# Expert rows added into h by scatters: a hybrid attention and mixture-of-experts block on one core

## The reference, cut to what matters

```
h = x + token_mixer(rms_norm(x, norm1_w), ...)
u = rms_norm(h, norm2_w)
# best of 4 groups, then the best 2 of its 8 experts; gate = softmax of the 2 scores * group weight
y[token, n] = (silu(u @ w_gate[e]) * (u @ w_up[e])) @ w_down[e]      # e: expert n of the token
h = h + sum over n of gate[token, n] * y[token, n]
out = rms_norm(h, final_norm_w)
```

## Time and profile before

| | |
|---|---|
| median of 3 runs | 1945.99 us (1945.32 to 1946.11) |
| profiled execution: its own time | 1948.25 us |
| profiled execution: span of the records | 1946.3 us |
| mean granted TensorE clock | 0.958 of full |
| mixer, about | 0 to 1009 us |
| routing, about | 1009 to 1063 us |
| experts | 1063 to 1863 us |
| last stage | 1863 to 1946 us |
| data moved by DMA | 379 MB, 195 GB/s over the span |

### The profile page before, as it was taken

One profiled execution on the slowest core, in us unless ns is written; L12 is line 12 of the kernel. 1 busy time (PEld: TensorE's weight loads), 2 busy tenths in 40 slices (PEclk: granted clock), 3 DMA queues, 4 the chain that ended last, 5 costly groups with the idle time before them and its releaser, 6 DMA issues.

```text
span 1946.3 us, 28769 instructions
## 1 busy us (share of the span) xinstructions
PE 1780.1 (91%) x10562; PEld 1267.3 (65%) x10563; DVE 572.6 (29%) x1111; ACT 498.9 (26%) x1189; POOL 216.1 (11%) x285
## 2 busy tenths in 40 slices
PE   7999999999999999999855999999999999999920
PEld 3566666566665666656634777888878778787710
DVE  1333233333233332433335111111111111111157
ACT  0434332343333342433310111111111111111113
POOL 0000001001011010110002000000000000000045
PEclk9999999999999999999976999999999999999965
DMA  9631133321333312333126789788998899898867
GB/s 322 188 109 61 59 97 108 108 83 36 97 108 108 104 39 73 108 108 108 64 90 235 273 290 325 267 299 308 322 316 296 299 314 329 286 332 303 281 221 319
DMA packets 231525, 379.01 MB, mean 195 GB/s; under 512 B 13715, under 2 KB 118180, under 8 KB 231492
## 3 DMA queue, kind: packets, MB, share of 16 engines
q1 hardware_dynamic: 220548, 340.14, 51.4%
q0 software_dynamic: 10944, 38.41, 5.9%
HBM read 282.04 MB, written 96.47 MB: 194 GB/s over the span
## 4 chain that ended last, share of the span: by engine, by line
PE 39%; DVE 4%; issue 4%; DMA 2%; ACT 1%; POOL 0%; SPq 0%; DVEq 0%; ACTq 0%; POOLq 0%
PE bank L1106 12%; PE bank L1131 12%; PE bank L1095 12%; PE bank L1120 1%; DMA out<-oc 1%; PE bank L1063 1%; DVE hT L1177 1%; DVE oc L1284 1%; DVE column L953 0%; DVE hc L1272 0%; DVE hc L1274 0%; ACT sg L1140 0%; DMA wts<-y_dram,dest 0%; DVE place L953 0%; PE bank L351 0%
## 5 line engine op out<-in xcount | busy, mean ns | idle before, releaser
L283 PE MATMUL bank<-w_in_sb,uT 128*128 128x512 f32 (+1 forms) x1024 | 381.7, 526 | 5.6 <-DMA w_in_sb<-w_in_in 5.6
L283 PEld LDWEIGHTS bank<-w_in_sb,uT 128*128 128x128 f32 x1024 | 177.3, 193 | 175.4 <-issue 168.5
L1095 PEld LDWEIGHTS bank<-xT,wts 128*128 128x128 f32 x2048 | 253.2, 194 | 28.9 <-issue 22.4
L1095 PE MATMUL bank<-xT,wts 128*128 128x128 f32 (+2 forms) x2048 | 258.7, 286 | 8.5 <-issue 6.6
L1106 PE MATMUL bank<-xT,wts 128*128 128x128 f32 (+2 forms) x2048 | 247.9, 282 | 0.0
L1106 PEld LDWEIGHTS bank<-xT,wts 128*128 128x128 f32 x2048 | 245.0, 191 | 0.0
L1131 PE MATMUL bank<-wts,hT 128*128 128x512 f32 x512 | 233.5, 599 | 3.8 <-DVE hT L1177 3.8
L431 PE MATMUL bank<-w_out_sb,mixT 128*128 128x512 f32 x512 | 224.2, 596 | 0.8 <-ACT mixT L508 0.8
L1177 DVE TENSOR_TENSOR hT<-bank,sg 128x256 f32<-128x256 f32 x128 | 54.3, 424 | 444.4 <-PE bank L1106 444.4
L431 PEld LDWEIGHTS bank<-w_out_sb,mixT 128*128 128x128 f32 x512 | 96.6, 191 | 116.9 <-issue 116.9
L1131 PEld LDWEIGHTS bank<-wts,hT 128*128 128x128 f32 x512 | 92.1, 190 | 105.6 <-issue 105.6
(11 more groups left out here) (212 smaller groups left out, 1714.6 us busy)
## 6 DMA issues: line engine op xcount, KB each, us to landing
wts<-w_gate_in SPq DMA_DIRECT2D x32, 2048.0 KB, 9.9
wts<-w_up_in SPq DMA_DIRECT2D x32, 2048.0 KB, 8.9
wts<-w_down_in SPq DMA_DIRECT2D x32, 2048.0 KB, 10.9
y_dram<-nought SPq DMA_DIRECT2D x96, 512.0 KB, 6.0
y_dram<-y SPq DMA_DIRECT2D x32, 512.0 KB, 9.7
x_sb<-x_in SPq DMA_DIRECT2D x17, 512.0 KB, 4.0
w_in_sb<-w_in_in SPq DMA_DIRECT2D x4, 2048.0 KB, 12.8
h_sb<-x_in SPq DMA_DIRECT2D x16, 512.0 KB, 6.3
```

The lines of the kernel that those rows point to most:

```text
L283: m = pe.matmul(bk[name][:, col:col + hi - lo], uT[:, k, :], w_in[:, k, lo:hi], start=k == 0, stop=k == KD - 1)
L1095: m = pe.matmul(G[m_ % 2][:, 0:w], wg[:, k, m_ * P:(m_ + 1) * P], xT[:, k, 0:w], start=k == 0, stop=k == KD - 1)
```

## The change

- Expert results no longer go through `y_dram`. ACT and VectorE scale by the gate of each slot (`gatec`, copied by ACT from `weight`) while they copy PSUM to `y`, and Pool adds the rows into h in DRAM with two indirect DMAs that accumulate (`put_back`). Empty slots add to spare rows behind h. One expert's scatters are waited for before the next one's go out (`scattered`), and that also frees `y`. The next expert's gather now follows the scatter in Pool's program.
- Routing makes two more tables per slot: `put` (the destination row) and `weight` (the gate). Pool writes the token products to a second tensor `column_t`, then multiplies `column` by the gates, four operations more; PE gets a second group of 32 matmuls and one more spread.
- `clear_y` is gone (two stores clear the spare rows), and so is the early load of h.
- The last stage loads h in four pieces after the last scatter has landed, normalises in place and stores.
- `sg` and `hT` are 160 columns wide in the main pass. Step 1 of the next expert's transposes stands before the down projection with step 0.
- Start: the bias of `qk` is loaded right behind the first `w_in` block, x of tile 1 behind the `v` block, five constants behind the `g` block, and six (with `alibi`) after all of `w_in`; their users wait for them where they need them.

```diff
+            if lo == C_QK:
+                sp.dma_start(b_tm[:, 0:C_V], A["b_in"][0:1, 0:C_V].to_broadcast([P, C_V])).then_inc(sem("b_qk_loaded"), 16)
             if lo == C_V:
-                for dst, src in [(b_tm[:, 0:C_LR], A["b_in"][0:1, 0:C_LR].to_broadcast([P, C_LR])),
+                sp.wait_ge(sem("xn_ready"), 1)
+                sp.dma_start(x[:, :], A["x"][P:2 * P, :]).then_inc(sem("x_loaded"), 16)
+            if lo == C_G:
...
+        for dst, src in [(sinks[:, :], A["swa_sinks"].to_broadcast([P, HB])),
+                         (gnorm[:, :], A["gla_norm_w"].to_broadcast([P, DV])),
+                         (cums[:, :, :], A["c_cums"]), (cind[:, :], A["c_cind"]),
+                         (causal[:, :], A["c_causal"]),
+                         (alibi[:, :, :], A["c_alibi"])]:
+            sp.dma_start(dst, src).then_inc(sem("late_consts"), 16)
...
-    def clear_y(sp, i):
-
-
-        blocks = scratch["y"].rearrange("(b p) (r c) -> b p r c", p=P, c=128)
+    def clear_spare(sp):
+
+        spare = scratch["h"][SEQ:SEQ + SPARE, :].rearrange("(b p) (r c) -> b p r c", p=P, c=128)
         src = nought[:, None, :].to_broadcast([P, D // 128, 128])
-        n = NE // NT
-        for m in range(n):
-            for b in (2 * (n * i + m) + 1, 2 * NE + 2 * (n * i + m), 2 * NE + 2 * (n * i + m) + 1):
-                dst = blocks[b] if isinstance(b, int) else blocks[bass.ds(b, 1)].rearrange("o p r c -> (o p) r c")
-                sp.dma_start(dst, src).then_inc(sem("y_cleared"), 16)
-
-    FIRST, CONSTS, W_OUT = 5 * 16, 11 * 16, 7 * 16
+        for b in range(SPARE // P):
+            sp.dma_start(spare[b], src).then_inc(sem("spare_cleared"), 16)
...
+            m = pe.matmul(bank[2][:, 0:NCOL], place[:, g, :], column_t[:, g, :], start=g == 0, stop=g == 2 * NT - 1)
+        m.then_inc(sem("slot_sums"), 1)
+        pe.wait_ge(sem("spread_args"), 1)
+        pe.matmul(bank[3][:, 0:NE], rep[:, 0:P], idx_f[:, :], start=True, stop=True).then_inc(sem("slot_sums"), 1)
+        for g in range(2 * NT):
+            if g % PART == 0:
+                pe.wait_ge(sem("columns_ready"), (2 * NT + g) // PART + 1)
+            m = pe.matmul(bank[6][:, 0:NCOL], place[:, g, :], column[:, g, :], start=g == 0, stop=g == 2 * NT - 1)
+        m.then_inc(sem("slot_sums"), 1)
+        pe.wait_ge(sem("spread_args"), 2)
+        pe.matmul(bank[7][:, 0:2 * NE], rep[:, 0:P], spread[:, :, :].rearrange("p a b -> p (a b)"), start=True, stop=True)\
+            .then_inc(sem("slot_sums"), 1)
...
+        pairs = lambda t: t.rearrange("p (n b) -> p n b", b=2)
+        link(dve.scalar_tensor_tensor(pairs(empty[:, :]), pairs(found), 0.0,
+                                      rep[:, None, P + 1:P + 3].to_broadcast([P, NCOL // 2, 2]), ALU.is_equal, ALU.mult))
+        link(dve.scalar_tensor_tensor(put_f[:, :], found, -1.0, empty[:, :], ALU.add, ALU.add))
+        dve.tensor_copy(put[:, 0:NCOL:2], put_f[:, 0:NCOL:2])
+        dve.tensor_copy(put[:, 2 * NE + 1:NCOL:2], put_f[:, 2 * NE + 1:NCOL:2])
+        dve.tensor_copy(spread[:, 0, :], put_f[:, 1:2 * NE:2])
+        v_.wait_ge(sem("slot_sums"), 3)
+        dve.tensor_copy(spread[:, 1, :], bank[6][:, 1:2 * NE:2]).then_inc(sem("spread_args"), 1)
+        dve.tensor_copy(weight[:, 0:NCOL:2], bank[6][:, 0:NCOL:2])
+        dve.tensor_copy(weight[:, 2 * NE + 1:NCOL:2], bank[6][:, 2 * NE + 1:NCOL:2])
+        v_.wait_ge(sem("slot_sums"), 4)
+        dve.tensor_scalar(put[:, 1:2 * NE:2], bank[7][:, 0:NE], 4.0, rep[:, P:P + 1], ALU.mult, ALU.add).then_inc(sem("puts_ready"), 1)
+        dve.tensor_copy(weight[:, 1:2 * NE:2], bank[7][:, NE:2 * NE]).then_inc(sem("puts_ready"), 1)
...
+            nc.gpsimd.tensor_tensor(column_t[:, g:g + PART, :], column[:, g:g + PART, :],
+                                    tok[:, t:t + PART].unsqueeze(2).to_broadcast([P, PART, NCOL]), ALU.mult)\
+                .then_inc(sem("columns_ready"), 1)
+        flat_gates = gates[:, :, :].rearrange("p n t -> p (n t)")
+        for n, g in enumerate(range(0, 2 * NT, PART)):
+            po.wait_ge(sem("columns_ready"), 2 * NT // PART + n)
             nc.gpsimd.tensor_tensor(column[:, g:g + PART, :], column[:, g:g + PART, :],
-                                    tok[:, t:t + PART].unsqueeze(2).to_broadcast([P, PART, NCOL]), ALU.mult)\
+                                    flat_gates[:, g:g + PART].unsqueeze(2).to_broadcast([P, PART, NCOL]), ALU.mult)\
                 .then_inc(sem("columns_ready"), 1)
...
+    def put_back(po, pre, src, col, quarters=False):
+
+        table = scratch["h"].rearrange("t (q c) -> (t q) c", q=4) if quarters else scratch["h"]
+        po.indirect_dma_start(out=table, out_offset=bass.IndirectOffsetOnAxis(ap=putc[:, col:col + 1], axis=0),
+                              in_=src, in_offset=None, compute_op=ALU.add).then_inc(sem(pre + "y_put"), 16)
+
+    def scatter(po, pre, n, col):
+
+        after(po, pre, "yA_taken", 2 * n + 2)
+        after(po, pre, "yD_taken", n + 1 if pre == "m_" else 2 * n + 2)
+        nc.gpsimd.tensor_copy(putc[:, :], put[:, bass.ds(col, 2)] if not isinstance(col, int) else put[:, col:col + 2])\
+            .then_inc(sem(pre + "put_index_ready"), 1)
+        wait_apart(po, meta_rider, (sem(pre + "put_index_ready"), n + 1))
+        put_back(po, pre, y[:, 0, :], 0)
+        if pre == "m_":
+            put_back(po, pre, yt, 1, quarters=True)
+        else:
+            put_back(po, pre, y[:, 1, :], 1)
+
+    def scattered(po, pre, n):
+
+        wait_apart(po, meta_rider, (sem(pre + "y_put"), 32 * n))
+        po.sem_inc(sem(pre + "y_free"), 1)
...
-        next_x((0,))
+        next_x((0, 1))
...
-                next_x((1, 2))
+                next_x((2,))
...
+        n_ = MAIN if pre == "m_" else CAP
         for m_ in range(KF):
             after(act, pre, "g_done", 4 * n + m_ + 1)
             after(act, pre, "h_ready", 4 * (n - 1) + m_ + 1)
-            act.activation(sg[:, m_, :], G[m_ % 2][:, 0:CAP], ACT.Silu).then_inc(sem(pre + "sg_ready"), 1)
-        wait(act, sem(f"{pre}y_stored"), 80 * (n + 1))
+            act.activation(sg[:, m_, 0:n_], G[m_ % 2][:, 0:n_], ACT.Silu).then_inc(sem(pre + "sg_ready"), 1)
+        after(act, pre, "yD_taken", n if pre == "m_" else 2 * n)
+        col = 2 * n if pre == "m_" else 2 * NE + 2 * n
+        act.activation(gatec[:, :], weight[:, bass.ds(col, 2)], ACT.Copy).then_inc(sem(pre + "gate_ready"), 1)
+        after(act, pre, "gate_ready", n + 1)
+        after(act, pre, "y_free", n)
         for part in (1, 0):
             after(act, pre, "d_done", 3 * n + 2 - part)
             if part and pre == "m_":
-                act.activation(yt, G[0][:, 0:CAP], ACT.Copy).then_inc(sem("m_yA_taken"), 1)
+                act.activation(yt, G[0][:, 0:CAP], ACT.Copy, scale=gatec[:, 1:2]).then_inc(sem("m_yA_taken"), 1)
...
+            nc.vector.tensor_tensor(hT[:, m_, 0:n_], U[m_ % 2][:, 0:n_], sg[:, m_, 0:n_], ALU.mult)\
...
-            wait(v_, sem(f"{pre}y_stored"), 80 * (n + 1))
+            after(v_, pre, "gate_ready", n + 1)
+            after(v_, pre, "y_free", n)
         after(v_, pre, "d_done", 3 * n + 3 - 2 * part)
-        nc.vector.tensor_copy(y[:, part, 512:D], (YB, G)[part][1][:, :]).then_inc(sem(pre + "yD_taken"), 1)
-
-    return (credit, load, store, store_over, gather, gather_over, copy_index, pe_x, pe_x_over, pe_chunk, act_chunk,
+        nc.vector.tensor_scalar(y[:, part, 512:D], (YB, G)[part][1][:, :], gatec[:, part:part + 1], None, ALU.mult)\
...
+    PIECES = ((0, 1), (1, 4), (4, 12), (12, 16))
+    h_rest = sb("h_rest", [P, 4, D])
+    hc = [W[:, t * D:(t + 1) * D] for t in range(NT - 4)] + [h_rest[:, t, :] for t in range(4)]
...
+        for n, (lo, hi) in enumerate(PIECES):
+            dst = W[:, lo * D:hi * D].rearrange("p (t d) -> p t d", d=D) if lo < NT - 4 else h_rest[:, :, :]
+            sp.dma_start(dst, scratch["h"][lo * P:hi * P, :].rearrange("(t p) d -> p t d", p=P)).then_inc(sem(f"h_back{n}"), 16)
         for t in range(NT):
             sp.wait_ge(sem("sum_o_ready"), t + 1)
-            sp.dma_start(A["out"][t * P:(t + 1) * P, :], oc[:, t % 2, :]).then_inc(sem(f"out_stored{t % 2}"), 16)
+            sp.dma_start(A["out"][t * P:(t + 1) * P, :], hc[t]).then_inc(sem("out_stored"), 16)
...
-            nc.vector.scalar_tensor_tensor(oc[:, t % 2, :], hc[:, t, :], fs[:, t, 1:2], fw[:, :], ALU.mult, ALU.mult)\
+            nc.vector.scalar_tensor_tensor(hc[t], hc[t], fs[:, t, 1:2], fw[:, :], ALU.mult, ALU.mult)\
                 .then_inc(sem("sum_o_ready"), 1)
...
-            with po.Fori(0, NE) as e:
+            po.sem_inc(sem("m_y_free"), CREDIT)
+            po.sem_inc(sem("o_y_free"), CREDIT)
+            for e in range(2):
                 copy_index(po, "m_", e, 2 * e)
                 gather(po)
-            copy_index(po, "m_", NE, 0)
-            gather(po)
+            po.wait_ge(sem("h_stored"), 16 * NT)
+            po.wait_ge(sem("spare_cleared"), 16 * SPARE // P)
```

(8 more changed lines are left out.)

194 lines of the change are left out of this document (76 added, 118 removed).

## The result

The changed kernel takes 1894.49 us (median of four runs, 1893.06 to 1896.23) against 1946.05 us (1945.32 to 1949.06) for the kernel before beside it: a ratio of 0.9733, 95% interval 0.9716 to 0.9749. That is 51.6 us less; the forecast was 31.5 us less. The sign was right, and the time lies 20 us under the forecast and 9.5 us under the lower end of its range. The profiled execution has a span of 1892.5 us, 53.8 less than the one of before.

| stretch | before | after | difference | forecast |
|---|---|---|---|---|
| start, to the first `qk` matmul of tile 1 | 59.04 | 52.45 | -6.6 | -5.5 |
| from there to the last logits | 949.75 | 949.09 | -0.7 | 0 |
| routing, to the first gate matmul | 54.24 | 58.82 | +4.6 | +6 |
| from there to the first silu table load | 3.90 | 2.17 | -1.7 | 0 |
| experts, first to last silu table load | 774.38 | 755.27 | -19.1 | -6 |

A forecast was written before the change was run, and what follows sets the result against it. PE, busy 91% of the span, was taken as the bound, with start, routing and last stage counting in full. Terms -5.5 + 6 - 6 - 26 = -31.5 gave a median of 1914.5 us, range 1904 to 1942.

The forecast's parts named there:

- Start: Start loads: the `w_in` block lands 5 us earlier, ending PE's wait ahead of `g`; 5.5 us less, bounds 0 to 6.3.
- so the wait costs 3.4 + 2.95: Ahead of `g`: PE's 3.4 us wait for `w_in` plus 2.95 us for matmuls slowed by the lowered clock, 6.3 us.
- Routing: Routing stage: Pool's four more gate multiplications delay the index copy and first gather; 6 us more, between 3.2 and 7.
- Experts: Expert stage: moved transposes and narrower `sg` and `hT` save 7.1 us, 1 taken back for the scatters; 6 us less.
- (a): Experts: four more transposes ahead of the down projection cover the 3.8 us wait for hT and 1.9 us idle.
- (b): Experts: `sg` and `hT` on 160 columns shorten silu by 0.08 us, taking 1.4 us from the waits for sg.
- rival A: Experts: adding scatters make the DMA engines the bound; 1975 us at 9 us a scatter pair; chance 0.13, plus 0.08 for about 1930.
- S: Experts: time of all 16 DMA engines for one expert's adding scatters, counted as 1.6 to 4.9 us; decides from 5.6.
- all hidden, with 5 us to spare: Experts: Pool's scatters and the next gather stay off PE's path; gather lands at 9.4 us, wanted at 14.6.
- Last stage: Last stage: h loads and stores on one queue end at 1915.5, plus 4.3 us close; 26 us less, bounds 20 to 30.
- B: Experts: the edits do nothing because waits for hT and sg only move to the next step; 1920.5 us, chance 0.13.
- C: Last stage: gains half, as stores run with gaps behind large loads or the scatter lands late; 1928 us, chance 0.09.

The follow-up runs named there:

- b_start: The kernel before with the new order of the start loads alone: 1941.57 us, ratio 0.9984.
- a_twice: The changed kernel with one more adding scatter of the 128 main rows (512 KB) of each expert: 1978.11 us, ratio 1.0184.
- b_three: The kernel before with the new start order, the transposes' new places and the 160 columns; routing, stores and last stage as before: 1929.03 us, ratio 0.9919.

## Why the prediction was right or wrong

**What bounds it** held: PE in the experts, the seams in full.

**Start** (-5.5). The profile gave -6.6, with the signs named: no wait ahead of `g`, full clock. But the term was summed against one execution whose wait had also cost it the clock. Two other executions of the old order show 54.1 and 54.4 for 59.04, and `b_start` 2.2 us by its median. The term is 2 to 3 for typical runs, and that the table agrees with 5.5 is luck; the step "so the wait costs 3.4 + 2.95" is right for the profiled run alone. The 0.7 us more up to the logits are within what other profiles with the same mixer show (948.6 to 950.3 us).

**Routing** (+6). +4.6. Between the bounds of 3.2 and 7 the value was taken too near to the upper one. GpSimd did not take turns over the whole: 7.91 us less the 4.0 that it had idle is 3.9. The other 0.7 is mostly the second sums, which the forecast had hidden: their spread held PE for 0.8 us behind the gather's landing. L985 and the cast L987 were stretched to 0.56 and 1.59 from 0.17 and 0.18, while L984, a reduce, kept its 0.97. The Trainium skill (SBUF — State Buffer, "Who interferes with whom") says that a cast or a `tensor_scalar` can take the shared port pair and a reduce never does; by that rule turns are taken at single instructions, and the trace agrees. What the forecast did not see is the 1.7 us given back ahead of the first table load, because the second sums kept PE's clock up.

**Experts** (-6). This is the step that failed, in two ways. (a) and (b) were mis-sized: "four transposes last 0.60 and the wait behind them is 0.21" took the idle column for all that the order would cover. It is 0.44 us for a narrow expert, not 0.21, and with the columns 0.55: 9.5 us in the last 23 periods and about 3.9 in the first eight (206.2 to 202.3, the means of two and of four profiles with 23 or 24 packets), 13.4 in all for a term of 7. Then the stops for instruction loads, a term put at nothing: 6.6 us of them stood in the trace of before, and the prediction neither counted them nor asked what moves them. The changed routing moved the experts' code by half a block, and 5.8 us of the first eight periods went with them in the profiles, 1 to 6 by whole times. The us taken back for the scatters was not needed: 558.4 us in the last 23 periods with them and 558.3 without.

**The adding scatter** (rival A) did not come. S is 1.9 us above a plain scatter and by `a_twice` about 2.6 for 512 KB; for the 640 KB of today an estimate is 3.3, below the 5.6 from which it was to decide. But "all hidden, with 5 us to spare" was wrong: the issue takes 1.6 us and not 0.96, the gather lands in 6.6 and not 4.4, and 1.3 us are left. The sentence that the gather "behind it on the same queue slips as well" named the right place; it, and not the weights, comes due first.

**Last stage** (-26). -30.3 here, and -29.7 from the last down matmul. The loads of h went out 9.9 us after that matmul, 10.5 forecast, and the DMA engines were done after 53, forecast 53.0. The failed term is the close: 4.3 us were carried over from before. In all ten profiles with the old stage the last DMA ended 4.7 us before the end, in all ten with the new one 0.7. What fills the 4.7 is GpSimd's closing drain: it starts with GpSimd's last operation, takes 8.7 us in each of the ten old ones and ends 0.24 us ahead of the span; in the new ones it takes 2.4 to 3.8 and ends 5 us or more ahead. Why it is so long with the old stage no run isolates.

**Rivals B and C** did not come: the edits gave more than expected, and the DMA engines held 417 GB/s over 30 us of the last stage.

## What to carry to other kernels

Size a reordering on the engine that bounds by start-to-start times of the same pieces, not by its idle column. A stop for "issue" in a loop with branches belongs in the account: it can change with an edit ahead of the loop that adds instructions, in steps that the edit's own work doesn't explain, so look at the packets of the instruction queue of both kernels before crediting an edit. And where a DMA is put behind others on GpSimd, count their issue and their landing against the spare time of the last one in the row.

## What was not expected of the hardware

- With PE's code moved by 132 or 160 instructions q8 had 19 packets and PE one to three stops, none behind the third expert; with 0 or 264 it had 23 or 24, and PE three or four stops, up to the ninth expert.
- Behind the ninth expert no profile has a packet of q8 until the experts are through, so what PE's loop needs is held by then, though PE goes on to branch between its widths.
- What a stop does to the clock is not settled by its length: behind stops of 1.51 and 1.96 us 64 matmuls of 160 columns took 8.96 and 10.63 us, but those of 128 columns took 9.03 behind one of 2.00 (the changed kernel) and 7.65 behind one of 2.12 (a repeat of `b_three`).
- An adding scatter takes 1.6 us of GpSimd's queue to issue, a gather 1.0, and its addition costs 3.3 us at the end of a chain and nothing in the experts.
- One more scatter of 512 KB cost 84 us in 32 experts, by delaying the gather behind it on GpSimd; the DMA engines' share stayed at 0.94.
- GpSimd's closing drain took 8.7 us with the old last stage and set the end of the span, 4.7 us behind the last DMA; with the new one it took 2.4 to 3.8.
